# Three seams of a two-layer decoder kernel: the operands of the next stage made before the last product of the stage in front

## The chip, the cores and the metric

The kernel runs on one core of a Trainium2 chip (trn2). The metric is the device time of one execution in microseconds. PE is TensorE, ACT is ScalarE, DVE is VectorE, POOL is GpSimd, SP is SyncE; PEld rows are the loads of weights into the array, which overlap the products.

## The reference, cut to what matters

Two layers over 256 tokens of width 1024. Each layer has a mixer sub-layer and then the channel sub-layer, in which every part of the change lies:

```python
def peer_ffn(h, w_q, sk1, sk2, u_tab, v_tab):      # h: normed and modulated (adaLN) input
    q = (t @ w_q).reshape(T, PEER_HEADS, 2, PEER_DKEY // 2)
    s1 = einsum('thd,kd->thk', q[:, :, 0], sk1); s2 = einsum('thd,kd->thk', q[:, :, 1], sk2)
    v1, i1 = top_k(s1, 16); v2, i2 = top_k(s2, 16)
    vc, ic = top_k(v1[..., :, None] + v2[..., None, :], 16)      # 16 of 128*128 experts, 8 heads
    gate = softmax(vc)
    a = einsum('td,thkd->thk', t, u_tab[expert])
    return einsum('thk,thkd->td', gate * gelu(a), v_tab[expert])
```

The kernel computes it without gathering: the product of `h` with all 16384 rows of `u_tab`, gelu, a multiplication with a dense grid of gates (zero where an expert was not picked), and the product of that grid with all of `v_tab`.

## The kernel before

All weights come as a stream of 512 KB blocks (128 x 1024 float32) through a ring of four slots, `ring`; SP issues the transfer of a block when the block four places ahead of it has been used. The order of work on each engine is written out by hand, and semaphores join the engines.

Products of the channel sub-layer are exact in two halves. Each operand is split in a rounded float32r part and a remainder (`h_hi`, `h_lo`; `split_hi`, `split_lo`; `w_hi`, `w_lo`), and PE makes three products for each (hi hi, hi lo, lo hi). ScalarE makes `split_hi` of a block (`high(n)`, L685), GpSimd or VectorE subtracts to get `split_lo` (L477, L1217, L1251). There are four slots of `split_hi` and `split_lo`.

The channel sub-layer of a layer goes like this:

- **Norm (seam A).** ScalarE squares the columns of x, PE sums them (`sums_of`, L1340) and then runs 36 filler products (`keep_running`), ScalarE takes the root (L516), having first split three blocks (L685). VectorE takes the reciprocal (L878) and multiplies eight slices of x by it into `sq` (L880). For each of eight slices k, ScalarE then applies scale and shift in place in `sq` (L693), and VectorE rounds it to `h_hi` (L1146) and subtracts to get `h_lo` (L1147). PE starts the query projection with slice 0 as soon as its two halves are there; slice k is waited for by `h_split`.
- **Queries and plain expert rows.** 16 query blocks, then 64 of the 128 blocks of `u_tab` ("rows", 24 products of 256 columns each). ScalarE follows in pairs of rows: it splits two further blocks and applies gelu to the pair (`gelu_pair`). Meanwhile VectorE does the top-k. Before the last four plain rows PE turns the picks (L1705) and ScalarE copies them to `pick` (L728).
- **Late rows (seam B in front of them).** The other 64 rows, each behind a group of four gate products (`gate_grids`, L1718): four tokens at a time, a one-hot of the first index times a one-hot of the second index gives that token's grid of gates. ScalarE makes the second one-hots (`column_hots(q)`: four Abs of 128 x 128, L736, and one Relu, L739), VectorE makes the first (`row_hots(q)`, L1202) and multiplies the gates into the gelus (`weigh(q)`, L1211 and L1212). There are 64 groups q and two buffers of one-hots. `column_hots(0)` and `column_hots(1)` stand behind the last plain `gelu_pair`. The gelus of the two rows that are just done go to `late_gelu` and are multiplied in by `weigh_late` (L1226).
- **Output rows (seam C in front of them).** 128 blocks of `v_tab`, each with 12 products of 512 columns (L1751) into banks 4 to 7 of PSUM, which add up over all blocks. Before them VectorE waits for all of `weigh_late`, clears `zeros` and signals `w_done`; PE multiplies `zeros` with `xT` in plain float32 to set the four banks to zero (L1741), ScalarE makes `w_hi` of the first four blocks of weights (L766) and VectorE `w_lo` (L1246). `w_hi` and `w_lo` lie over `h_hi`. The first four `v_tab` blocks were split as the last four of the early sequence (`high`, `late_low`). In the first layer, each 20 output rows are followed by column sums for the second layer's adaLN (`ada_sums`, L1353), whose input VectorE adds up in `ada_step` from a second ring, `ada_ring`.

Of the kernel before, what the change touches and what calls it, by code (L numbers as in the profile page):

```python
# [18 lines left out]
F32 = mybir.dt.float32  # L19
# [145 lines left out]
def build(nc, stream, s5w, consts, mixc, small, vec, pos, x_in, out):  # L165
    with ExitStack() as ctx:
# [11 lines left out]
        def at_byte(name, at, shape, dt=F32):  # L178
            return nc.alloc_sbuf_tensor_at(name, [P] + shape, dt, offset=base + at, align_bytes=32)
# [11 lines left out]
        h_hi = at_byte("h_hi", 48 * KB, [KT, T], F32R)  # L191
        w_hi = at_byte("w_hi", 48 * KB, [SPLIT, T], F32R)
        w_lo = at_byte("w_lo", 52 * KB, [SPLIT, T], F32R)
        y_rows = at_byte("y_rows", 48 * KB, [TT, D])
# [9 lines left out]
        late_gelu = at_byte("late_gelu", 67 * KB, [2, 2, T])  # L204
        zeros = at_byte("zeros", 72 * KB, [P])
        ynT = at_byte("ynT", 72 * KB, [KT, T])
# [7 lines left out]
        mod2 = sb("mod2", [P, DEPTH, ADA])  # L214
        tiny = sb("tiny", [P, 216])

# [65 lines left out]
        onehot = g(120 * T, 2048)  # L282
        qT = sq

        tpos = [0]
# [21 lines left out]
        posc = tn(2)  # L307
        epst = tn(1)
        zero = tn(1)
        drel = at_byte("drel", 70 * KB + 512, [(BUCKETS - 1) * HEADS])  # L310
# [83 lines left out]
        vhi_ready, v_ready, v_used = sem("vhi_ready"), sem("v_ready"), sem("v_used")  # L394
        turned_picks, w_done = sem("turned_picks"), sem("w_done")
        spill = nc.dram_tensor("spill", (P, HEADS * (P + T) + 3 * T), F32).ap()
# [13 lines left out]
        def _(sp):  # L410
# [26 lines left out]
            for l in range(DEPTH):  # L437
# [7 lines left out]

                sp.wait_ge(w_done, l + 1)
                with sp.Fori(0, ADA // KT, 1) as i:
# [48 lines left out]
        def _(act):  # L496
# [55 lines left out]
            for l in range(DEPTH):  # L552
# [170 lines left out]
                gelus(6)  # L723
                for j in range(4):
                    if j == 2:
                        act.wait_ge(turned_picks, l + 1)
                        for i in range(TT):
                            nc.scalar.activation(pick[:, :, i * P:i * P + P], bank[:, 6 + i, 0:3 * P].rearrange("p (r t) -> p r t", r=3),  # L728
                                                 ACT.Copy).then_inc(pick_ready, 1)
                    gelu_pair(7, j)  # L730

                def column_hots(q):
# [8 lines left out]

                act.wait_ge(pick_ready, TT * (l + 1))
                for q in range(2):
                    column_hots(q)
# [41 lines left out]
        def _(dve):  # L786
# [82 lines left out]
            for l in range(DEPTH):  # L869
# [350 lines left out]
                def weigh_late(p):  # L1220
# [6 lines left out]
                        .then_inc(late_done, 1)  # L1227

                for q in range(2):
# [12 lines left out]
                v.memset(zeros[:, :], 0.0).then_inc(w_done, 1)  # L1242
                late = early_at(l) + EARLY
                for j in range(SPLIT):
                    dve.wait_ge(vhi_ready, l * KEYS + j + 1)
                    v.tensor_tensor(w_lo[:, j, :], grid[:, j * T:j * T + T], w_hi[:, j, :].bitcast(F32), ALU.subtract).then_inc(v_ready, 1)  # L1246

# [50 lines left out]
        def _(pe):  # L1298
# [79 lines left out]
            for l in range(DEPTH):  # L1378
# [358 lines left out]

                pe.wait_ge(w_done, l + 1)
                pe.wait_ge(late_lo, (l + 1) * DVE_LOWS)
                for b4 in range(4):  # L1740
                    mm(bank[:, 4 + b4, :], zeros[:, :], xT[:, 0:2, :], start=True, stop=False, skip_group_check=True)  # L1741

                def output_rows(i, n, a0):

                    for j in range(n):
                        s = (a0 + j) % SPLIT
                        pe.wait_ge(v_ready, i * n + (l * KEYS + a0 + j + 1))
                        for r in range(TT):
                            for half_w, half_v in ((w_hi, split_hi), (w_hi, split_lo), (w_lo, split_hi)):
                                for c in range(2):  # L1750
                                    last = mm(bank[:, 4 + 2 * r + c, :], half_w[:, s, r * P:r * P + P],  # L1751
                                              half_v[:, s, c * 512:c * 512 + 512], start=False, stop=False, skip_group_check=True)
                        last.then_inc(v_used, 1)

                if l + 1 < DEPTH:
                    with pe.Fori(0, ADA // KT, 1) as i:
                        output_rows(i, 20, 0)
                        pe.wait_ge(ada_used, i * KT + ((l + 1) * ADA + KT))
                        ada_sums(0, i, ada_acc)
                    output_rows(0, 8, 120)  # L1760
                else:
                    with pe.Fori(0, KEYS // SPLIT, 1) as i:
                        output_rows(i, SPLIT, 0)

# [142 lines left out]
```

## Time and profile before

| | us |
|---|---|
| median of 3 runs | 2254.84 (2251.26 to 2256.5) |
| the profiled execution, its own time | 2254.05 |
| span of the profile | 2252.3 |
| PE busy | 2140.1 (95%) |
| DVE busy | 1547.3 (69%) |
| ACT busy | 1226.8 (54%) |
| POOL busy | 440.0 (20%) |
| mean granted clock of TensorE | 0.979 of full |

The span is 1.75 us shorter than the execution's own time. The first layer's channel sub-layer runs from about 289 to 1180 us of the span, the second's from about 1358 to 2240 us. A timeline row gives start and length in us, the engine, the line, the operation, output and input, and in brackets how long the engine sat idle before it and what ended that. A group "x4" is one row for four instructions in a row.

### The profile page before, as it was taken

The page shows a single profiled execution, that of the slowest core. Times are in us where ns is not written, and L with a number is a line of the kernel's source. Part 1 is how long each engine was busy: PE and PEld are TensorE (multiplying, and loading weights), DVE is VectorE, ACT ScalarE, POOL GpSimd, SP SyncE. Part 2 cuts the span into 40 slices and gives each one's busy share as a digit, 9 for nine tenths or more (in the row PEclk, how much of TensorE's full clock was granted, in tenths as well). Part 3 has the DMA queues.
Part 4 walks back from the last instruction along what each step waited for, and adds up shares of the span by engine and source line. Part 5 has one row for each costly group of instructions (what it writes and reads, how often), then busy time and mean ns, then how long its engine had stood idle before and what let it go on. Part 6 is the DMA issues. An engine that isn't in the chain of part 4 may idle for free.

```text
span 2252.3 us, 39908 instructions
## 1 busy us (share of the span) xinstructions
PE 2140.1 (95%) x13732; PEld 1947.7 (86%) x13732; DVE 1547.3 (69%) x3026; ACT 1226.8 (54%) x2330; POOL 440.0 (20%) x184
## 2 busy tenths in 40 slices
PE   5799999999999999999999989999999999999997
PEld 4688789999999978888878978999999997888886
DVE  7688458991678867777758945899168885555555
ACT  8623434555788844444443343454578884554553
POOL 0000056898000000000000005689800000000000
PEclk9799999999999999999999999999999999999999
DMA  7723244545444457777763323445544444555552
GB/s 261 277 85 122 95 133 140 169 165 189 131 132 147 133 174 262 261 261 262 258 208 117 122 75 133 140 168 168 187 132 138 142 135 140 192 195 194 190 193 102
DMA packets 103475, 378.80 MB, mean 168 GB/s; under 512 B 11488, under 2 KB 11872, under 8 KB 102880
## 3 DMA queue, kind: packets, MB, share of 16 engines
q1 hardware_dynamic: 102672, 373.74, 49.4%
q10 hardware_dynamic: 720, 4.00, 0.5%
q8 instruction: 46, 0.75, 0.1%
q14 instruction: 37, 0.30, 0.0%
HBM read 375.46 MB, written 2.23 MB: 168 GB/s over the span
## 4 chain that ended last, share of the span: by engine, by line
PE 72%; issue 9%; POOL 7%; DVE 5%; DMA 3%; ACT 2%; SPq 0%; POOLq 0%; DVEq 0%; ACTq 0%
PE bank L1751 29%; PE bank L1654 8%; PE bank L1655 8%; PE bank L1656 8%; POOL split_lo L477 7%; PE bank L1718 5%; PE bank L1391 4%; DMA ring<-stream 2%; PE bank L1403 1%; PE bank L1642 1%; PE bank L1353 1%; DMA ada_ring<-stream 1%; DVE grid L855 1%; ACT split_hi L685 1%; PE bank L1427 1%
## 5 line engine op out<-in xcount | busy, mean ns | idle before, releaser
L1654 PE MATMUL bank<-h_hi,split_hi 128*128 128x256 f32 x2304 | 668.7, 290 | 25.2 <-POOL split_lo L477 11.1
L1655 PE MATMUL bank<-h_lo,split_hi 128*128 128x256 f32 x2304 | 653.9, 284 | 0.0
L1656 PE MATMUL bank<-h_hi,split_lo 128*128 128x256 f32 x2304 | 653.8, 284 | 0.0
L1251 DVE TENSOR_TENSOR split_lo<-ring,split_hi 128x1024 fp32r<-128x1024 f32 x248 | 303.8, 1225 | 251.3 <-ACT w_hi L773 251.3
L1654 PEld LDWEIGHTS bank<-h_hi,split_hi 128*128 128x128 f32 x2304 | 443.7, 193 | 32.0 <-POOL split_lo L477 16.8
L477 POOL TENSOR_TENSOR split_lo<-ring,split_hi 128x1024 fp32r<-128x1024 f32 x168 | 433.2, 2603 | 175.4 <-ACT split_hi L685 175.2
L772 ACT ACTIVATE split_hi<-ring 128x1024 fp32r<-128x1024 f32 x248 | 263.2, 1061 | 361.6 <-PE bank L1751 361.6
L1655 PEld LDWEIGHTS bank<-h_lo,split_hi 128*128 128x128 f32 x2304 | 444.4, 193 | 0.0
L1656 PEld LDWEIGHTS bank<-h_hi,split_lo 128*128 128x128 f32 x2304 | 443.6, 193 | 0.0
L685 ACT ACTIVATE split_hi<-ring 128x1024 fp32r<-128x1024 f32 x296 | 298.6, 1051 | 211.9 <-PE bank L1656 211.8
L1751 PE MATMUL bank<-split_hi,w_hi 128*128 128x512 f32 x1024 | 316.9, 391 | 0.0
L1751 PE MATMUL bank<-split_lo,w_hi 128*128 128x512 f32 x1024 | 315.4, 389 | 0.0
L1751 PE MATMUL bank<-split_hi,w_lo 128*128 128x512 f32 x1024 | 315.3, 389 | 0.0
L1751 PEld LDWEIGHTS bank<-split_hi,w_hi 128*128 128x128 f32 x1024 | 191.8, 188 | 40.6 <-issue 1.2
L1751 PEld LDWEIGHTS bank<-split_lo,w_hi 128*128 128x128 f32 x1024 | 192.2, 188 | 40.1
L1751 PEld LDWEIGHTS bank<-split_hi,w_lo 128*128 128x128 f32 x1024 | 192.2, 188 | 40.0
L1217 DVE TENSOR_TENSOR split_lo<-ring,split_hi 128x1024 fp32r<-128x1024 f32 x128 | 151.1, 1221 | 98.8 <-ACT split_hi L685 98.8
L470 POOL TENSOR_TENSOR tiny<-tiny,K 128x1 f32<-128x1 f32 x12 | 6.6, 549 | 1019.2 <-DVE tiny L1056 1019.2
L1202 DVE TENSOR_SCALAR hots<-K,pick 128x128 f32<-128x128 f32 x512 | 145.6, 346 | 61.9 <-ACT pick L728 61.9
L736 ACT ACTIVATE hots<-K,pick 128x128 f32<-128x128 f32 x512 | 163.6, 394 | 23.4 <-PE bank L1718 23.4
L1718 PE MATMUL bank<-hots 128*128 128x128 f32 x1024 | 136.7, 277 | 9.0 <-ACT hots L739 9.0
L1718 PEld LDWEIGHTS bank<-hots 128*128 128x128 f32 x1024 | 126.9, 193 | 9.3 <-issue 9.3
(273 smaller groups left out, 2546.2 us busy)
## 6 DMA issues: line engine op xcount, KB each, us to landing
ring<-stream SPq DMA_DIRECT2D x658, 512.0 KB, 3.4
ada_ring<-stream SPq DMA_DIRECT2D x48, 512.0 KB, 4.3
spill<-tables ACTq DMA_DIRECT2D x1, 1152.0 KB, 4.3
tables<-spill ACTq DMA_DIRECT2D x1, 1152.0 KB, 7.1
xT<-x_in SPq DMA_DIRECT2D x1, 1024.0 KB, 9.6
s5raw<-s5w ACTq DMA_DIRECT2D x2, 512.0 KB, 5.6
y_out<-hT SPq DMA_DIRECT2D x1, 1024.0 KB, 3.9
KM<-mixc SPq DMA_DIRECT2D x1, 576.0 KB, 7.6
```

Of the source, the lines that this page charges most:

```text
L477: gp.tensor_tensor(split_lo[:, j, :], ring[:, (e0 + j) % RING, :], split_hi[:, j, :].bitcast(F32), ALU.subtract)\
L685: nc.scalar.activation(split_hi[:, n % SPLIT, :], ring[:, (e0 + n) % RING, :], ACT.Copy).then_inc(hi_ready, 1)
L736: last = nc.scalar.activation(hotB[q % 2][:, t, :], iota, ACT.Abs, scale=-1.0, bias=pick[:, 1, at:at + 1])
L772: nc.scalar.activation(split_hi[:, j, :], ring[:, s, :], ACT.Copy)
L1202: last = v.tensor_scalar(hotA[q % 2][:, t, :], iota, pick[:, 0, at:at + 1], pick[:, 2, at:at + 1], ALU.is_equal, ALU.mult)
L1217: v.tensor_tensor(split_lo[:, e % SPLIT, :], ring[:, (early_at(l) + e) % RING, :], split_hi[:, e % SPLIT, :].bitcast(F32), ALU.subtract).t ...
L1251: v.tensor_tensor(split_lo[:, s, :], ring[:, (late + j) % RING, :], split_hi[:, s, :].bitcast(F32), ALU.subtract)
L1654: mm(dst, hi, x_hi, start=start, stop=False, skip_group_check=not group)
L1655: mm(dst, hi, x_lo, start=False, stop=False, skip_group_check=not group)
L1656: return mm(dst, lo, x_hi, start=False, stop=stop, skip_group_check=not group)
L1718: last = mm(bank[:, 4 + q % 4, t * P:t * P + P], hotB[q % 2][:, t, :], hotA[q % 2][:, t, :], start=True, stop=True)
L1751: last = mm(bank[:, 4 + 2 * r + c, :], half_w[:, s, r * P:r * P + P], half_v[:, s, c * 512:c * 512 + 512], start=False, stop=False, skip_g ...
```

## The change

Four edits, all in the channel sub-layer, in both layers:

1. *h in two forms.* ScalarE writes each slice twice: rounded, straight into `h_hi`, and in full into a new place `h_full`; VectorE only subtracts. The rounding on VectorE, and a wait of VectorE on itself behind it, are gone. A one-element Sqrt on ScalarE (`junk`) stands ahead of the three early splits.
2. *One-hot columns.* `column_hots(0)` and `column_hots(1)` stand ahead of the last plain `gelu_pair`.
3. *First weights' halves.* `w_hi` and `w_lo` of the first four blocks are made in the turn of the last late pair (`weights_high`, `weights_low`), behind a wait for all 64 groups of gates, and lie where the one-hots lay (72 KB).
4. *No zero products.* `zeros` and its products are gone; the first output row starts the sums. PE no longer waits for `w_done`, but for `w_ready` and block by block for `late_lo`. The first four output rows stand ahead of the loop, so the adaLN sums come after 24, 44, ... output rows. ScalarE's and SP's later parts wait for `late_done`.

```diff
@@ ScalarE
+                nc.scalar.activation(junk, epst, ACT.Sqrt)
                 for n in range(SPLIT - 1):
                     high(n)
                 root(l, "ss2", D, rstd)
                 for k in range(KT):
                     act.wait_ge(xr_ready, 2 * KT * l + KT + k + 1)
-                    nc.scalar.activation(sq[:, k, :], sq[:, k, :], ACT.Identity, bias=mod2[:, l, 3 * KT + k:3 * KT + k + 1],
-                                         scale=sc2[:, k:k + 1]).then_inc(h_ready, 1)
+                    for dst in (h_hi, h_full):
+                        last = nc.scalar.activation(dst[:, k, :], sq[:, k, :], ACT.Identity,
+                                                    bias=mod2[:, l, 3 * KT + k:3 * KT + k + 1], scale=sc2[:, k:k + 1])
+                    last.then_inc(h_ready, 1)
                 high(SPLIT - 1)
...
+                    if j == 3:
+                        act.wait_ge(pick_ready, TT * (l + 1))
+                        for q in range(2):
+                            column_hots(q)
+                    gelu_pair(7, j)
+
+                def weights_high():
+
+                    act.wait_ge(w_ready, QUADS * (l + 1))
+                    for j in range(SPLIT):
+                        nc.scalar.activation(w_hi[:, j, :], grid[:, j * T:j * T + T], ACT.Copy).then_inc(vhi_ready, 1)
...
+                    if p == LATE_PAIRS - 1:
+                        weights_high()
                     act.wait_ge(a_ready, first + FIRST_LATE // 2 + p + 1)
                     for w in range(2):
                         high(PQ + a0 + w + SPLIT)
...
-                act.wait_ge(w_done, l + 1)
+                act.wait_ge(late_done, LATE_PAIRS * (l + 1))
                 late = e0 + EARLY
-                for j in range(SPLIT):
-                    nc.scalar.activation(w_hi[:, j, :], grid[:, j * T:j * T + T], ACT.Copy).then_inc(vhi_ready, 1)
@@ VectorE
                     dve.wait_ge(h_ready, 2 * KT * l + KT + k + 1)
-                    link(v.tensor_copy(h_hi[:, k, :], sq[:, k, :]))
-                    v.tensor_tensor(h_lo[:, k, :], sq[:, k, :], h_hi[:, k, :].bitcast(F32), ALU.subtract).then_inc(h_split, 1)
+                    v.tensor_tensor(h_lo[:, k, :], h_full[:, k, :], h_hi[:, k, :].bitcast(F32), ALU.subtract).then_inc(h_split, 1)
...
+                    if p == LATE_PAIRS - 1:
+                        weights_low()
                     for w in range(2):
                         late_low(POOL_LOWS + 2 * p + w)
                     weigh_late(p)
...
-                v.memset(zeros[:, :], 0.0).then_inc(w_done, 1)
@@ TensorE
-                pe.wait_ge(w_done, l + 1)
-                pe.wait_ge(late_lo, (l + 1) * DVE_LOWS)
-                for b4 in range(4):
-                    mm(bank[:, 4 + b4, :], zeros[:, :], xT[:, 0:2, :], start=True, stop=False, skip_group_check=True)
+                pe.wait_ge(w_ready, QUADS * (l + 1))
...
+                for j in range(SPLIT):
+                    pe.wait_ge(v_ready, l * KEYS + j + 1)
+                    pe.wait_ge(late_lo, (l + 1) * DVE_LOWS - SPLIT + j + 1)
+                    output_row(j, first=j == 0)
                 if l + 1 < DEPTH:
                     with pe.Fori(0, ADA // KT, 1) as i:
-                        output_rows(i, 20, 0)
+                        output_rows(i, 20, SPLIT)
```

## Rows read from the trace of the kernel before

**Rows 1.** Page, part 1: engine, busy us, share of the span, instructions.

```profile
PE 2140.1 (95%) x13732; PEld 1947.7 (86%) x13732; DVE 1547.3 (69%) x3026; ACT 1226.8 (54%) x2330; POOL 440.0 (20%) x184
```

**Rows 2.** Windows: busy us of PE, PEld, DVE, ACT, POOL; PEclk, DMA share, GB/s.

```profile
301.00:310.00 9.00, 6.68 (x33) 5.68 (x34) 6.42 (x14) 3.09 (x5) 2.46 (x1) 0.81 0.17 60
...
570.00:807.00 237.00, 237.00 (x2016) 237.00 (x2016) 188.10 (x463) 192.16 (x429) 0.00 (x0) 1.00 0.42 137
820.00:1100.00 280.00, 280.00 (x1277) 233.24 (x1276) 198.88 (x239) 136.66 (x200) 0.00 (x0) 1.00 0.73 259
```

**Rows 3.** Timeline of the norm in the first layer (seam A).

```profile
289.76 2.93 ACT L685 ACTIVATE split_hi<-ring 128x1024 fp32r<-128x1024 f32 x3
290.88 7.17 POOL L477 TENSOR_TENSOR split_lo<-ring,split_hi 128x1024 fp32r<-128x1024 f32 x3 [29.27 <-ACT split_hi L685]
...
292.60 0.45 ACT L516 ACTIVATE grid<-bank,tiny 128x256 f32<-128x256 f32 x1
...
294.94 5.39 DVE L880 TENSOR_TENSOR grid<-xT,grid 128x256 f32<-128x256 f32 x8
...
298.36 3.55 ACT L693 ACTIVATE grid<-grid,mod,tiny 128x256 f32<-128x256 f32 x7 [1.89 <-DVE grid L880]
...
303.23 2.45 DVE L1147 TENSOR_TENSOR h_lo<-grid,h_hi 128x256 fp32r<-128x256 f32 x1
...
305.73 0.38 PE L1654 MATMUL bank<-h_hi,split_hi 128*128 128x256 f32 x1 [2.07 <-DVE h_lo L1147]
...
307.24 0.42 DVE L1147 TENSOR_TENSOR h_lo<-grid,h_hi 128x256 fp32r<-128x256 f32 x1
...
308.77 0.38 ACT L511 ACTIVATE grid<-bank 128x256 f32<-128x256 f32 x1 [5.91 <-PE bank L1656]
```

**Rows 4.** Timeline of ScalarE from the last plain pairs into the late rows, first layer.

```profile
550.33 0.86 ACT L728 ACTIVATE pick<-bank 128x384 f32<-128x384 f32 x2
...
556.26 0.58 ACT L711 ACTIVATE grid<-bank 128x512 f32<-128x512 f32 x1
...
562.49 1.26 ACT L736 ACTIVATE hots<-K,pick 128x128 f32<-128x128 f32 x4
563.78 0.63 ACT L739 ACTIVATE hots<-hots 128x512 f32<-128x512 f32 x1
...
576.30 0.16 ACT L758 ACTIVATE late_gelu<-bank 128x16 f32<-128x16 f32 x1
```

**Rows 5.** Timeline, PE's first two groups of gates: first layer, then second.

```profile
564.56 2.04 PE L1718 MATMUL bank<-hots 128*128 128x128 f32 x8 [4.49 <-ACT hots L739]
...
570.42 1.05 PE L1718 MATMUL bank<-hots 128*128 128x128 f32 x8
...
1633.52 1.64 PE L1718 MATMUL bank<-hots 128*128 128x128 f32 x8 [4.49 <-ACT hots L739]
...
1638.90 1.06 PE L1718 MATMUL bank<-hots 128*128 128x128 f32 x8
```

**Rows 6.** Timeline of seam C in the first layer.

```profile
805.64 0.16 DVE L1212 COPY grid<-bank 128x8 f32<-128x8 f32 x1
...
809.00 2.36 DVE L1217 TENSOR_TENSOR split_lo<-ring,split_hi 128x1024 fp32r<-128x1024 f32 x2 [3.20 <-ACT split_hi L685]
...
812.25 1.33 ACT L766 ACTIVATE w_hi<-grid 128x256 fp32r<-128x256 f32 x4 [1.85 <-DVE zeros L1242]
...
812.27 6.62 PE L1741 MATMUL bank<-xT,zeros 128*128 128x512 f32 x8 [4.40 <-DVE zeros L1242]
...
818.33 1.02 PE L1751 MATMUL bank<-split_hi,w_hi 128*128 128x512 f32 x2
```

**Rows 7.** Timeline of seam C in the second layer, PE alone.

```profile
1880.76 6.57 PE L1741 MATMUL bank<-xT,zeros 128*128 128x512 f32 x8 [4.40 <-DVE zeros L1242]
1886.76 1.03 PE L1751 MATMUL bank<-split_hi,w_hi 128*128 128x512 f32 x2
```

**Rows 8.** Waits of PE from 1098 to 1160 us: us in total, times, longest.

```profile
PE bank L1353 <- DVE ada_acc L1264: 1.2, 1, 1.2
```

More of the change, by code:

```diff
@@ L191, in build @@
         h_hi = at_byte("h_hi", 48 * KB, [KT, T], F32R)
-        w_hi = at_byte("w_hi", 48 * KB, [SPLIT, T], F32R)
-        w_lo = at_byte("w_lo", 52 * KB, [SPLIT, T], F32R)
+        w_hi = at_byte("w_hi", 72 * KB, [SPLIT, T], F32R)
+        w_lo = at_byte("w_lo", 76 * KB, [SPLIT, T], F32R)
         y_rows = at_byte("y_rows", 48 * KB, [TT, D])
@@ L204, in build @@
         late_gelu = at_byte("late_gelu", 67 * KB, [2, 2, T])
-        zeros = at_byte("zeros", 72 * KB, [P])
         ynT = at_byte("ynT", 72 * KB, [KT, T])
@@ L214, in build @@
         mod2 = sb("mod2", [P, DEPTH, ADA])
-        tiny = sb("tiny", [P, 216])
+        tiny = sb("tiny", [P, 217])
         g3 = grid[:, :].rearrange("p (a t) -> p a t", a=KEYS)
@@ L283, in build @@
         qT = sq
+        h_full = g(8192, KT, T)
         tpos = [0]
@@ L308, in build @@
         epst = tn(1)
+        junk = tn(1)
         zero = tn(1)
@@ L394, in build @@
         vhi_ready, v_ready, v_used = sem("vhi_ready"), sem("v_ready"), sem("v_used")
-        turned_picks, w_done = sem("turned_picks"), sem("w_done")
+        turned_picks = sem("turned_picks")
         spill = nc.dram_tensor("spill", (P, HEADS * (P + T) + 3 * T), F32).ap()
@@ L444, in _ @@
                     break
-                sp.wait_ge(w_done, l + 1)
+                sp.wait_ge(late_done, LATE_PAIRS * (l + 1))
                 with sp.Fori(0, ADA // KT, 1) as i:
@@ L723, in _ @@
                 gelus(6)
[L724 to L730, printed above, removed]
                 def column_hots(q):
@@ L740, in column_hots @@
                         .then_inc(column_ready, 1)
-                act.wait_ge(pick_ready, TT * (l + 1))
-                for q in range(2):
-                    column_hots(q)
+                for j in range(4):
+                    if j == 2:
+                        act.wait_ge(turned_picks, l + 1)
+                        for i in range(TT):
+                            nc.scalar.activation(pick[:, :, i * P:i * P + P], bank[:, 6 + i, 0:3 * P].rearrange("p (r t) -> p r t", r=3),
+                                                 ACT.Copy).then_inc(pick_ready, 1)
+                    if j == 3:
[7 more added lines that the diff above has]
+                        nc.scalar.activation(w_hi[:, j, :], grid[:, j * T:j * T + T], ACT.Copy).then_inc(vhi_ready, 1)
                 for p in range(LATE_PAIRS):
@@ L1227, in weigh_late, with weights_low @@
                         .then_inc(late_done, 1)
+                def weights_low():
+                    for j in range(SPLIT):
+                        dve.wait_ge(vhi_ready, l * KEYS + j + 1)
+                        v.tensor_tensor(w_lo[:, j, :], grid[:, j * T:j * T + T], w_hi[:, j, :].bitcast(F32), ALU.subtract)\
+                            .then_inc(v_ready, 1)
                 for q in range(2):
@@ L1241, in _ @@
                 dve.wait_ge(late_done, LATE_PAIRS * (l + 1))
-                v.memset(zeros[:, :], 0.0).then_inc(w_done, 1)
                 late = early_at(l) + EARLY
-                for j in range(SPLIT):
-                    dve.wait_ge(vhi_ready, l * KEYS + j + 1)
-                    v.tensor_tensor(w_lo[:, j, :], grid[:, j * T:j * T + T], w_hi[:, j, :].bitcast(F32), ALU.subtract).then_inc(v_ready, 1)
                 def low(i, n, j):
@@ L1736, in _, with output_row @@
                     late_rows(i, False)
-                pe.wait_ge(w_done, l + 1)
-                pe.wait_ge(late_lo, (l + 1) * DVE_LOWS)
-                for b4 in range(4):
-                    mm(bank[:, 4 + b4, :], zeros[:, :], xT[:, 0:2, :], start=True, stop=False, skip_group_check=True)
+                pe.wait_ge(w_ready, QUADS * (l + 1))
+                def output_row(s, first=False):
+                    for r in range(TT):
+                        for n, (half_w, half_v) in enumerate(((w_hi, split_hi), (w_hi, split_lo), (w_lo, split_hi))):
+                            for c in range(2):
+                                last = mm(bank[:, 4 + 2 * r + c, :], half_w[:, s, r * P:r * P + P],
+                                          half_v[:, s, c * 512:c * 512 + 512], start=first and n == 0, stop=False, skip_group_check=True)
+                    last.then_inc(v_used, 1)
@@ L1743, in output_rows @@
                 def output_rows(i, n, a0):
                     for j in range(n):
-                        s = (a0 + j) % SPLIT
                         pe.wait_ge(v_ready, i * n + (l * KEYS + a0 + j + 1))
[L1748 to L1752, printed above, removed]
@@ L1753, in output_rows @@
-                        last.then_inc(v_used, 1)
+                        output_row((a0 + j) % SPLIT)
+                for j in range(SPLIT):
+                    pe.wait_ge(v_ready, l * KEYS + j + 1)
+                    pe.wait_ge(late_lo, (l + 1) * DVE_LOWS - SPLIT + j + 1)
+                    output_row(j, first=j == 0)
                 if l + 1 < DEPTH:
                     with pe.Fori(0, ADA // KT, 1) as i:
-                        output_rows(i, 20, 0)
+                        output_rows(i, 20, SPLIT)
@@ L1758, in _ @@
                         pe.wait_ge(ada_used, i * KT + ((l + 1) * ADA + KT))
                         ada_sums(0, i, ada_acc)
-                    output_rows(0, 8, 120)
+                    output_rows(0, LATE - 120, SPLIT + 120)
                 else:
-                    with pe.Fori(0, KEYS // SPLIT, 1) as i:
-                        output_rows(i, SPLIT, 0)
+                    with pe.Fori(0, LATE // SPLIT, 1) as i:
+                        output_rows(i, SPLIT, SPLIT)
                 pe.wait_ge(y_copied, 2 * TT * (l + 1))
```

## The prediction

> **What bounds the kernel now.** I read the page first: PE is busy for 95% of the span and no other engine for more than 69% [rows 1]. So the time is PE's work plus PE's holes, and the change, which takes almost no work from PE, must be judged by the holes. The windows come second: from 570 to 807 us (late rows) and from 820 to 1100 us (output rows) PE is busy in every microsecond at a granted clock of 1.00, which is the 2.4 GHz level [rows 2]. There, nothing on another engine matters. What is left are three seams in each layer, read in the timeline.
>
> *Seam A* [rows 3]. The root ends at 293.05. VectorE's eight multiplications take 5.39 us and end at 300.33, since GpSimd's three subtractions run until 298.05; a VectorE operation of two inputs beside a GpSimd subtraction takes long (one `h_lo` took 2.45 us against 0.42). That one leaves PE idle for 2.07 us. VectorE's last `h_lo` ends at 307.66, and PE's first query row is ready for ScalarE at 308.77. From 301 to 310 us the granted clock was 0.81 on average [rows 2].
>
> *Seam B* [rows 5]. PE ends the last plain row at 564.56 - 4.49 = 560.07, waits 4.49 us for the first one-hot columns, and then runs the gates and half a row at the lower clock: the first gates take 2.04 us, the second 1.05. The second gates start at 570.42.
>
> *Seam C* [rows 6]. PE ends the last late row at 812.27 - 4.40 = 807.87, waits 4.40 us, spends 6.06 us on the zero products, and starts the output rows at 818.33.
>
> **The change part by part.**
>
> *C, no zero products and early halves.* The output rows can start when three things are there. (1) All gates weighed: `weigh(63)` ends at 805.80 [rows 6]. (2) The halves of the first weights. ScalarE's four copies take 1.33 us [rows 6] and end near 807.2; VectorE follows each with a subtraction of the shape of `h_lo`, 0.42 us [rows 3], so the first is ready near 805.85 + 0.4 + 0.42 = 806.7, the fourth near 807.7. ScalarE is idle then: it waits for the last late pair. (3) The halves of the first two `v_tab` blocks, which belong to the pair before. So PE goes on at 807.87. Blocks 2 and 3 are split at 809.00 to 811.36 as before [rows 6]; what is queued behind the new wait on `w_ready` on ScalarE are these two splits, which could not start before 807.9 anyway, since they wait for the last late row. One output row takes about 2.75 us: in 280 us there are 1277 matmul records [rows 2], of which 80 are five times the adaLN sums, so 1197/12 = 100 rows, 280/100 = 2.8 with the sums. Block 2 is needed at 807.9 + 5.5 = 813.4 and is there at 810.2; block 3 at 816.1 against 811.4. Block 4 waits for ScalarE, which waits for `late_done` (near 812), then split and copy and VectorE's two subtractions, some 3.1 us: 815.2, needed at 818.9. SP's first further transfer goes with it; it comes 7.3 us after the first output row starts, and its block is needed 22 us after. Gain: 818.33 - 807.87 = 10.46 in the first layer, 1886.76 - (1880.76 - 4.40) = 10.40 in the second [rows 7]. **20.9 us.** Its floor is the zero products alone, if PE still had to wait as long: 6.06 + 6.00 = 12.1.
>
> *B, one-hot columns early.* Picks are copied by 551.2 and ScalarE is free from 556.84, after the pair before the last [rows 4]. A set of columns takes 1.26 + 0.63 us less overlap, near 1.85: ready at 558.7 and 560.5 [rows 4]. PE needs the first at 560.07 and the second one row later. What is now queued behind the second set are the two splits of the last plain pair, which began at 560.10 and now begin at 560.5: 0.4 late, for rows that PE reaches at 568 or later; GpSimd's subtractions behind them end near 566.3. Behind the gelu of that pair (near 563) VectorE weighs group 0 and makes the row one-hots of group 2, near 565 to 566, needed at 567.9. What is saved is exact: a gate group and a row take (812.27 - 4.40 - 570.42)/63 = 3.77 us in steady work, and the second group would start at 560.07 + 3.77 = 563.84 and not at 570.42: 6.58. In the second layer 1638.90 - (1629.03 + 3.77) = 6.10 [rows 5]. **12.7 us.** Its floor is the two idle stretches without the clock's part, 9.0.
>
> *A, h in two forms.* VectorE drops eight roundings, but ScalarE now makes two activations per slice. Seven took 3.55 us [rows 3], so fourteen take 7.10; both of slice 0 fit in the gap before 298.36. ScalarE ends at 305.46. The added Sqrt is nearest to the activation of 16 columns, 0.16 us [rows 4]; below, nothing, if it overlaps. It delays the three splits, the root behind them (ScalarE goes from one to the other without a gap) and the chain: I take 0.1. The last `h_lo` ends at 305.56 + 0.42 = 306.0 instead of 307.66. The fourth split moves behind the sixteen activations (to 305.6), so GpSimd's fourth subtraction no longer meets the `h_lo` chain: the 2.45 us case is gone. Its block is needed two rows later, near 312.5, and is there near 309. Gain per layer: 1.7 by this, and up to 0.4 more if the last products run at the full clock. Against it: writes in the rounded form might not overlap as the seven did. At the full-width 0.60 each fourteen take 8.4, and the gain is 0.4. The clock is the other unknown. Before, PE worked in short bursts and the clock fell behind the 2.07 us hole. Now it gets one slice (three products) per 1.0 us for five slices. If the clock falls at the end of that, the next row runs at half speed for up to 3 us, 1.4 lost. I take 1.6 per layer, **3.2 us**; ends -2 and +5 for both layers.
>
> The Trainium skill, "TensorE: Matmul & The Clock Gate", section "A second HAM failure mode: psum-queue depth-cycling", tells of a kernel whose matmul groups had brief idles between them and whose clock went back and forth between its two levels. By this the thin stretch of seam A would end in the lower clock; that is the first rival below. The trace shows a drop only behind real holes here; a stretch fed as thinly as the new one is in no row.
>
> *adaLN sums four rows later.* One wait of 1.2 us, in the first layer's last turn, is for `ada_step` being late [rows 8]. With four more rows in front, 11 us, it goes: **1.2 us**, at worst 0. In return VectorE's first `ada_step` of the next turn waits for the sums, some 1.4 us in each of five turns; its next block is then ready some 5 us before PE needs it. No cost.
>
> **Sum.** 20.9 + 12.7 + 3.2 + 1.2 = 38.0. The profiled execution took 2254.05, which gives 2216.05. The median of the runs is 0.79 above that execution: 2216.8, rounded 2217.
>
> **The rivals.**
>
> *1. The clock falls at seam A.* Gain there between -1 and 0.3 per layer instead of 1.6: 2220 to 2222. For it: the thin feed; against it: seams A before had idles as well and recovered within 3 us.
>
> *2. The cover of seam C or B is too thin.* At C the margin between the first `w_lo` (806.7) and 807.87 is 1.2 us. If ScalarE's copies came behind the last late pair after all, PE would wait 4.4 us again in each layer and only the zero products would be saved: 2217 + 8.8 = 2226. Against it: `weigh(63)` at 805.80 in the trace.
>
> *3. The gain of B is given back in the late rows.* PE moves 6.6 us ahead of ScalarE and VectorE, which are busy for 192 and 188 of 237 us [rows 2]. If they can't follow, PE waits until the old spacing is back: 2217 + 12.7 = 2230. Against it: everything that they do is released by PE's own signals, and they have 45 us of idle time to catch up.
>
> *4. The other side: without its pauses TensorE is granted less clock.* The pauses at B and C go, and PE works without a hole from 301 to 1180 us and from 1370 to 2236 us, some 1750 us. To end slower than 2254.84 by 0.2%, 38 + 4.5 = 42.5 us must be lost: 1750 (1/x - 1) = 42.5 at a clock of x = 0.976. At 0.95 it would cost 92 us: 2309. Against it: 237 us and 280 us without any pause at 1.00 [rows 2].
>
> **How the numbers follow.** A run of this kernel tells a change of about 0.2% (4.5 us) from none. Forecast 0.66; rival 1 0.15; rival 2 0.09; rival 3 0.05; rival 4 0.04; no measurable change, by something that I don't see, 0.01. All but the last two are faster: 0.95, same 0.01, slower 0.04. The range: below, seam A at +5 (1.8 under the sum) and the spread of the runs, whose fastest is 3.6 under their median: 2211.5. Above, rival 1 and the floor of B or rival 2: 2226.
>
> **What would show it.** In the new profile: no L1741 rows; the first output product within 0.3 us of the last late product; the first gates start near 560 at 1.05 us, not at 564.56 at 2.04; all `h_lo` at 0.42 us and 16 activations in about 8 us; no wait for `ada_acc`; PE busy time some 13 us lower for the zero products, and a few us for the clock. Wrong would be: PE idle before the first output row over 1 us; a wait at the third or fifth output row; PE waits inside the late rows; granted clock under 1.00 in the long stretches.

## The result, and the profile after

The changed kernel takes 2213.76 us (median of 4 runs, 2213.12 to 2216.07); the kernel before, in the same comparison, 2253.87. The ratio is 0.9824 with a 95% interval of 0.9811 to 0.9838: 40 us faster. The forecast was 2217.0, with a range of 2211.5 to 2226. Of all executions below, one, of the version with late halves, took 11902 us; it counts in no ratio.

The page of the changed kernel, part 1 (busy us, share of the span, instructions), answers to [rows 1]:

```profile
span 2211.3 us, 39875 instructions
...
PE 2118.7 (96%) x13716; PEld 1934.7 (87%) x13716; DVE 1543.2 (70%) x3008; ACT 1234.4 (56%) x2348; POOL 440.1 (20%) x184
```

PE has 16 rows fewer, the zero products, and is busy for 21.4 us less. The span is 41.0 us shorter, so about half of it was busy time (zero products, and work at the lower clock) and half was idle.

The windows (columns as in [rows 2]) of the three seams in both layers, and of the long stretches behind them:

```profile
300.00:310.00 10.00, 8.54 (x63) 7.70 (x63) 2.48 (x7) 7.98 (x14) 4.61 (x2) 1.00 0.11 31
1347.00:1358.00 11.00, 9.39 (x57) 8.58 (x58) 2.81 (x8) 7.76 (x15) 4.72 (x2) 0.84 0.17 54
555.00:566.00 11.00, 11.00 (x96) 11.00 (x95) 6.56 (x13) 9.93 (x22) 6.32 (x3) 1.00 0.60 192
...
796.00:808.00 12.00, 12.00 (x60) 10.14 (x60) 8.21 (x12) 7.21 (x12) 0.00 (x0) 1.00 0.48 169
...
560.00:796.00 236.00, 236.00 (x2008) 236.00 (x2007) 191.42 (x469) 193.81 (x434) 2.60 (x2) 1.00 0.44 141
800.00:1150.00 350.00, 350.00 (x1593) 291.38 (x1592) 247.74 (x299) 169.34 (x248) 0.00 (x0) 1.00 0.75 261
```

Seams B (third row) and C (fourth) are full. Seam A is not: PE is idle for 1.5 us of ten in the first layer and for 1.6 of eleven in the second. The granted clock stayed at 1.00 there in the first layer and fell to a mean of 0.84 in the second.

The timeline of seam A in the first layer, against [rows 3]:

```profile
288.66 0.19 ACT L689 ACTIVATE tiny<-tiny 128x1 f32<-128x1 f32 x1
288.75 2.93 ACT L686 ACTIVATE split_hi<-ring 128x1024 fp32r<-128x1024 f32 x3
289.87 7.18 POOL L478 TENSOR_TENSOR split_lo<-ring,split_hi 128x1024 fp32r<-128x1024 f32 x3 [29.62 <-ACT split_hi L686]
...
293.94 5.41 DVE L891 TENSOR_TENSOR grid<-xT,grid 128x256 f32<-128x256 f32 x8
...
303.78 0.58 ACT L696 ACTIVATE grid<-grid,mod,tiny 128x256 f32<-128x256 f32 x1
...
304.40 0.43 DVE L1157 TENSOR_TENSOR h_lo<-grid,h_hi 128x256 fp32r<-128x256 f32 x1 [0.56 <-ACT grid L696]
...
305.54 0.38 ACT L512 ACTIVATE grid<-bank 128x256 f32<-128x256 f32 x1 [0.22 <-PE bank L1671]
```

The last `h_lo` ends 16.5 us behind the last square (start 288.34), where it took 18.2 before (307.66 - 289.44). ScalarE sets the pace: the last activation ends and the last subtraction starts 0.04 us later. VectorE's eight multiplications still take 5.4 us beside GpSimd.

Seam B in the first layer, ScalarE and VectorE, then PE, against [rows 4, 5]:

```profile
553.04 1.27 ACT L732 ACTIVATE hots<-K,pick 128x128 f32<-128x128 f32 x4
554.35 0.63 ACT L735 ACTIVATE hots<-hots 128x512 f32<-128x512 f32 x1
...
556.72 1.99 ACT L686 ACTIVATE split_hi<-ring 128x1024 fp32r<-128x1024 f32 x2
...
559.97 3.23 DVE L1212 TENSOR_SCALAR hots<-K,pick 128x128 f32<-128x128 f32 x4
```

```profile
556.21 1.06 PE L1733 MATMUL bank<-hots 128*128 128x128 f32 x8
...
559.98 1.06 PE L1733 MATMUL bank<-hots 128*128 128x128 f32 x8
563.75 1.06 PE L1733 MATMUL bank<-hots 128*128 128x128 f32 x8
```

The columns are ready before PE ends its plain rows, the first gates run at the full clock, and the groups follow each other at 3.77 us from the first. The VectorE row is the close one: four row one-hots took 3.23 us beside GpSimd's subtractions (one of the four alone 2.44) and ended at 563.20, for gates at 563.75. The second layer has the same margin of 0.55 us.

Seam C in the first layer, against [rows 6]:

```profile
795.20 0.16 DVE L1222 COPY grid<-bank 128x8 f32<-128x8 f32 x1
795.85 1.43 DVE L1243 TENSOR_TENSOR w_lo<-grid,w_hi 128x256 fp32r<-128x256 f32 x4 [0.48 <-ACT w_hi L754]
798.57 2.36 DVE L1227 TENSOR_TENSOR split_lo<-ring,split_hi 128x1024 fp32r<-128x1024 f32 x2 [1.29 <-ACT split_hi L686]
```

```profile
797.28 0.63 PE L1760 MATMUL bank<-split_hi,w_hi 128*128 128x512 f32 x2
```

All four `w_lo` are there at 797.28, when PE begins its output rows, and PE waits for none of them.

**Where the 41.0 us of the span went.** The same marks are read in both timelines: last square, ScalarE's copy of the second query row, copy of the picks, first `late_gelu`, copy of the finished sums to `y_rows`.

| stretch | layer 1: before, after | layer 2: before, after | gain |
|---|---|---|---|
| last square to second query row (A) | 22.65, 20.07 | 22.28, 21.55 | 3.3 |
| to the copy of the picks | 238.24, 238.23 | 238.41, 238.37 | 0.1 |
| to the first late gelu (B) | 25.97, 19.22 | 25.48, 19.23 | 13.0 |
| to the finished sums (C and the adaLN sums) | 603.34, 590.88 | 590.77, 579.80 | 23.4 |

Ahead of the first square, between the layers and behind the last sums, where nothing was changed, the two profiles differ by 1.1 us together, nearly all of it at the start. That makes 40.9, the 41.0 of the span but for rounding.

The table sets one execution against one. How long the kernel before takes at seams A and C differs from profile to profile. Over the ten profiled layers with the old seam A (before, b_only, c_only, b_fill, b_fill18) the stretch takes 22.3 to 23.3 us, 22.8 in the mean; over the ten with h in two forms and late early splits (after, a_only, halves_late, four_back, no_sqrt) it takes 20.0 to 21.6, 20.5 in the mean. So edit 1 is worth some 4.6 us for both layers, and the 3.3 of this pair is at the low end.

### The profile page after: what moved, and what is told of

The parts are those of the page before. It is cut to its first block, busy times and chain, and to the rows that moved or that the text cites. A ratio compares the mean times of both kernels' runs of the same rounds, so it can differ in the third digit from the quotient of the medians.

```text
span 2211.3 us, 39875 instructions
## 1 busy us (share of the span) xinstructions
PE 2118.7 (96%) x13716; PEld 1934.7 (87%) x13716; DVE 1543.2 (70%) x3008; ACT 1234.4 (56%) x2348; POOL 440.1 (20%) x184
## 4 chain that ended last, share of the span: by engine, by line
PE 74%; issue 9%; POOL 8%; DVE 4%; ACT 2%; DMA 2%; POOLq 0%; ACTq 0%; SPq 0%; DVEq 0%
PE bank L1760 32%; PE bank L1669 8%; PE bank L1670 8%; PE bank L1671 8%; POOL split_lo L478 7%; PE bank L1733 5%; PE bank L1406 4%; DMA ring<-stream 2%; PE bank L1418 1%; PE bank L1657 1%; PE bank L1368 1%; ACT diag L536 1%; PE bank L1431 1%; PE bank L1442 1%; PE bank L1379 1%
## 5 line engine op out<-in xcount | busy, mean ns | idle before, releaser
L1669 PE MATMUL bank<-h_hi,split_hi 128*128 128x256 f32 x2304 | 666.5, 289 | 23.3 <-POOL split_lo L478 11.1
L1212 DVE TENSOR_SCALAR hots<-K,pick 128x128 f32<-128x128 f32 x512 | 150.4, 360 | 61.9 <-ACT pick L742 61.9
```

The lines of the kernel that those rows point to most:

```text
L1212: last = v.tensor_scalar(hotA[q % 2][:, t, :], iota, pick[:, 0, at:at + 1], pick[:, 2, at:at + 1], ALU.is_equal, ALU.mult)
L1669: mm(dst, hi, x_hi, start=start, stop=False, skip_group_check=not group)
```

## The experiments

All ratios are against the kernel before, run on the same chip. A stretch is named by the letters of the table.

**Each part alone.** Edit 1 in the kernel before (h in two forms and the Sqrt; the diffs are cut to what matters):

```diff
+                    for dst in (h_hi, h_full):
+                        last = nc.scalar.activation(dst[:, k, :], sq[:, k, :], ACT.Identity, ...)
+                    last.then_inc(h_ready, 1)
```

> Edit 1 alone (h in two forms, with the one-element Sqrt) in the kernel before. Theory 1, each part fills its own hole in PE's work and the parts add: the profiles of before and after give 2.6 us in the first layer and 0.8 in the second, 3.4 together, so a ratio near 0.9985. Theory 2, the parts share a gain (PE arriving earlier at one seam waits longer at the next): the holes at seams B and C would be longer than 4.49 and 4.40 us and nothing would be left, ratio 1.000. The clock: if the thin feed of slices alone is enough to lower it, the query row after seam A runs at the lower clock in at least one layer.

Measured: 2247.55 us, ratio 0.9974 (0.9962 to 0.9985). A is 20.07 in both layers, 4.8 us less together, more than expected: this time the clock did not fall in either layer, so the query row at the lower clock, which was expected in at least one, did not come. C did not change its length before the first weights' halves (235.96 from the first late gelu, against 235.95), so nothing is given back there. B is 26.49 and 26.46, 0.5 to 1.0 longer than before, at the same wait.

Edit 2 in the kernel before:

```diff
+                    if j == 3:
+                        act.wait_ge(pick_ready, TT * (l + 1))
+                        for q in range(2):
+                            column_hots(q)
                     gelu_pair(7, j)
```

> Edit 2 alone (one-hot columns ahead of the last plain gelus). Theory 1: 6.75 + 6.25 = 13.0 us, ratio 0.9942, and the hole at seam C stays at 4.40 us. Theory 2 (given back in the late rows or at seam C): the hole at C grows by what B gained, ratio over 0.998.

Measured: 2240.46 us, ratio 0.9945 (0.9929 to 0.9962). B is 19.22 in both layers, and the stretch from the first late gelu to the first weights' halves is 235.96, as in the kernel before. That is theory 1: nothing is given back.

Edits 3 and 4, by undoing 1 and 2 in the changed kernel:

```diff
-                    if j == 3:
-                        act.wait_ge(pick_ready, TT * (l + 1))
-                        for q in range(2):
-                            column_hots(q)
                     gelu_pair(7, j)
+                act.wait_ge(pick_ready, TT * (l + 1))
+                for q in range(2):
+                    column_hots(q)
```

> Edits 3 and 4 alone (halves of the first weights early, no zero products, adaLN sums after 24, 44, ... rows). Theory 1: 10.6 + 10.6, 0.4 per layer for the first products at the full clock and 1.2 to 1.5 for the adaLN sum, 23.2 us, ratio 0.9897. Theory 2: under 15 us, ratio over 0.993, with new waits of PE inside the first output rows.

Measured: 2229.54 us, ratio 0.9894 (0.9878 to 0.9911). C is 590.88 and 579.81, as in the changed kernel to 0.01 us. The three parts sum to 4.8 + 13.0 + 23.4 = 41.2 us by their stretches; together they gave 39.7. The difference of 1.5 us is seam A of the second layer, where the clock fell.

**The two halves of seam C.** Halves of the first weights behind the last late pair, still without zero products:

```diff
                 act.wait_ge(late_done, LATE_PAIRS * (l + 1))
+                weights_high()
@@ and on VectorE
                 dve.wait_ge(late_done, LATE_PAIRS * (l + 1))
+                weights_low()
```

> The changed kernel, but the halves of the first weights made after the last late pair again; the zero products stay out. It tells the two halves of seam C apart. Theory 1: PE waits from the last late product for the last multiplication of the late pair (4.1 us) and then for one copy and one subtraction (1 us), 5.2 us a layer, and starts at the lower clock for 2 to 3 us (1 to 1.5 more): 12 to 13 us slower than the changed kernel, ratio to before 0.988. Theory 2, that the zero products were the whole price and the early halves are worth nothing: same as the changed kernel, 0.982.

Measured: 2228.13 us, ratio 0.9887 (0.9867 to 0.9906). C is 6.8 and 7.0 us longer than in the changed kernel, 13.8 together. PE's timeline in the first layer:

```profile
803.81 1.20 PE L1758 MATMUL bank<-split_hi,w_hi 128*128 128x512 f32 x2 [5.17 <-issue]
804.80 1.06 PE L1758 MATMUL bank<-split_lo,w_hi 128*128 128x512 f32 x2
805.65 1.06 PE L1758 MATMUL bank<-split_hi,w_lo 128*128 128x512 f32 x2
...
807.55 0.62 PE L1758 MATMUL bank<-split_hi,w_lo 128*128 128x512 f32 x2
```

A hole of 5.17 us, and then pairs of products at 1.06 us until the clock is back and they take 0.62. The first output row (twelve products) takes 4.20 and 4.40 us, against 2.75 in the changed kernel. So each layer loses the hole and 1.45 to 1.65 us of lower clock behind it. Without the early halves, edits 3 and 4 are worth 9.6 of the 23.4 us, the adaLN sums' 1.4 included.

**The price of the four products.** In front of the output rows of the changed kernel:

```diff
+                for b4 in range(4):
+                    mm(bank[:, 4 + b4, :], ident, xT[:, 0:2, :], start=True, stop=True)
```

> The changed kernel with four plain float32 products of the shape of the zero products back in front of the output rows (operands: the identity and x; the first output row overwrites what they leave, so the sums are those of the changed kernel). It prices the four products when PE comes to them at the full clock. Before they took 6.06 us behind a hole. Theory 1: their price was mostly the lower clock, so here 3.0 to 3.5 us a layer, 6 to 7 us in all over the changed kernel, ratio to before 0.985. Theory 2, their price doesn't hang on the clock: 12 us, ratio 0.9876.

Measured: 2221.95 us, ratio 0.9854 (0.9837 to 0.987). C is 3.46 us longer in each layer (594.34 and 583.26). PE's timeline in the first layer:

```profile
799.12 3.60 PE L1755 MATMUL bank<-xT,K 128*128 128x512 f32 x8
802.15 1.02 PE L1762 MATMUL bank<-split_hi,w_hi 128*128 128x512 f32 x2
```

From the start of the four products to the start of the first output product it is 3.03 us. The other 0.42 lies in the first output product, which has to let the last of the four end: the first pair takes 1.02 us here, as it did behind the zero products [rows 6], and 0.63 in the changed kernel. The lower clock is not the reason, in neither kernel. The windows of the kernel before (columns as in [rows 2]), over the zero products and from the first output product on:

```profile
812.00:818.00 6.00, 5.73 (x7) 2.52 (x8) 1.60 (x5) 1.33 (x4) 0.00 (x0) 0.50 0.46 160
818.30:821.50 3.20, 3.20 (x15) 2.44 (x13) 0.00 (x0) 0.00 (x0) 0.00 (x0) 1.00 0.00 0
```

So at the full clock four plain float32 products of 512 columns cost 3.46 us. Behind the hole of the kernel before they cost 6.06 [rows 6] and the same 0.42, 6.5 in all. In the ten profiled layers with zero products, always behind 4.40 us of idle time, start to start they took 4.65 to 6.06 us, by how much of them ran at the lower clock. So of the 13 us that the zero products cost in the first profile, 6 belonged to the hole in front of them.

**The clock at seam B.** Filler products in the hole of the kernel before, first 36, then 18:

```diff
+                for _ in range(36):
+                    mm(bank[:, 4, 0:P], ident, ones, start=True, stop=True)
                 late_rows(0, True)
```

> The kernel before with 36 filler products of 128 columns in the hole of seam B (bank 4, which the first gates overwrite), nothing moved. It splits B's gain into the wait and the clock. Theory 1: the wait of 4.49 us stays, but the first gates and the first late row run at the full clock: 2.1 + 1.6 = 3.7 us less, ratio 0.9984. Theory 2, the clock's part is no part of its own: ratio 1.000.

Measured: 2256.52 us, ratio 1.0009 (1.0000 to 1.0019), a miss by a wrong count: a plain float32 product stands as two rows in the profile, so the fillers lasted not 4.1 but 8.2 us and became the path themselves. B is 27.26 in both layers. The norm's own 36 fillers had stood as 72 rows and 8.20 us in the trace of the kernel before.

```profile
562.51 8.20 PE L1735 MATMUL bank<-K 128*128 128x128 f32 x72
570.55 1.06 PE L1718 MATMUL bank<-hots 128*128 128x128 f32 x8
```

> The kernel before with 18 filler products (36 rows of 0.114 us, 4.1 us) in the hole of seam B, half of what stood in the run with 36, whose 72 rows took 8.2 us and were longer than the hole. Theory 1, seam B is a wait of 4.49 us plus the lower clock behind it: the stretch from the copy of the picks to the first late gelu, 25.5 to 26.5 us before and 19.2 after, is 19.2 + 4.5 = 23.7 here in both layers. Theory 2, the clock has no part: 25.5 or more.

Measured: 2250.2 us, ratio 0.9983 (0.9974 to 0.9993). B is 23.95 and 23.96, against 25.5 to 26.5 in the six profiled layers where this seam was neither filled nor moved (before, a_only and c_only) and 19.22 with early columns. With the fillers the granted clock of the seam is 1.00. So seam B was a wait of 4.7 us and 1.5 to 2.5 us of lower clock behind it. The numbers of the two theories lay apart, and the first holds.

**The one-element Sqrt.** Taken out of the changed kernel:

```diff
-                nc.scalar.activation(junk, epst, ACT.Sqrt)
```

> The changed kernel without the one-element Sqrt. Theory 1: no table load hangs on it (none stands before the root of this norm in either profile), so it costs its 0.1 us a layer: same as the changed kernel, root 0.1 us earlier. Rival: without it a load of 1.28 us appears before the root, 2.6 us slower.

Measured: 2213.83 us, ratio 0.9811 (0.9794 to 0.9827). The root comes 3.17 us behind the last square and not 3.25, and there is no table load in front of it in either kernel. It costs 0.1 us a layer and gives nothing. A in the second layer is 21.47: the clock fell here too.

**GpSimd beside VectorE.** The three early splits between the last squares:

```diff
+                for m in range(KT):
+                    act.wait_ge(dve_taken, taken_count(l, f"out{m}")[1])
+                    nc.scalar.activation(sq[:, m, :], xT[:, m, :], ACT.Square).then_inc(sq_ready, 1)
+                    if m >= 5:
+                        if l == 0 and m == 5:
+                            act.wait_ge(spilled, 16)
+                        high(m - 5)
                 nc.scalar.activation(junk, epst, ACT.Sqrt)
-                for n in range(SPLIT - 1):
-                    high(n)
```

> The changed kernel with the three early splits of ScalarE spread between the last squares instead of behind them (and the Sqrt left out of the way of the root is gone with them only in place: it now stands behind the squares). GpSimd then ends its three subtractions before VectorE's eight multiplications. Theory 1, VectorE is held up by GpSimd: the eight take 2.7 us instead of 5.4, ScalarE's first gap goes, and seam A ends 1.5 to 2 us earlier in each layer: 3 to 4 us less than the changed kernel, ratio 0.9808. Rival: ScalarE waits for a block at its ring slot and delays the squares, so that nothing is won: 0.9824.

Measured: 2206.88 us, ratio 0.9789 (0.9773 to 0.9805). Its timeline in the first layer:

```profile
290.32 2.35 POOL L478 TENSOR_TENSOR split_lo<-ring,split_hi 128x1024 fp32r<-128x1024 f32 x1 [1.11 <-ACT split_hi L681]
...
294.19 2.77 DVE L892 TENSOR_TENSOR grid<-xT,grid 128x256 f32<-128x256 f32 x8
```

GpSimd is through before VectorE begins, the eight multiplications take 2.77 us and not 5.41, and A is 17.79 in both layers: 2.3 us less than the undisturbed 20.07. The median is 6.9 us below the changed kernel's, where 3 to 4 were expected: in the profiles 4.6 are these two stretches, and 1.5 the clock, which did not fall in either layer here.

With that in place, the first edit undone:

```diff
-                    for dst in (h_hi, h_full):
-                        last = nc.scalar.activation(dst[:, k, :], sq[:, k, :], ACT.Identity, ...)
+                    nc.scalar.activation(sq[:, k, :], sq[:, k, :], ACT.Identity, ...).then_inc(h_ready, 1)
@@ and on VectorE
+                    link(v.tensor_copy(h_hi[:, k, :], sq[:, k, :]))
```

> The changed kernel with the early splits, but h in one form (edit 1 undone, no Sqrt). It tells whether edit 1 is worth anything when GpSimd's first three subtractions are out of the way. Theory 1, half of edit 1's gain was that GpSimd's fourth subtraction no longer met the h_lo chain: here it meets it again (ScalarE is through after 8 activations, near 299.7, and GpSimd starts while VectorE has four slices to go), one h_lo takes 2.4 us, and seam A is 1 to 2 us longer than with both: 18.9 to 19.8. Rival: VectorE's 0.66 us per slice beats ScalarE's 0.98 and seam A is 0.9 us shorter: 16.9.

Measured: 2213.6 us, ratio 0.9821 (0.9805 to 0.9838). A is 20.39 in both layers, 2.6 longer than with two forms. The row that decides:

```profile
298.24 2.37 POOL L478 TENSOR_TENSOR split_lo<-ring,split_hi 128x1024 fp32r<-128x1024 f32 x1 [7.04 <-ACT split_hi L681]
298.38 2.51 DVE L1156 TENSOR_TENSOR h_lo<-grid,h_hi 128x256 fp32r<-128x256 f32 x1
```

The fourth GpSimd subtraction meets the `h_lo` chain again: one subtraction takes 2.51 us, and the query row behind it 3.82 us instead of 2.88, by the clock. So what counts in edit 1 is the moved fourth split, and not ScalarE's speed: in one form the last `h_lo` ends 15.5 us behind the last square, of which some 2.1 are the held subtraction, and in two forms 14.2. No run moves the fourth split alone, so that one form would then be the shorter is worked out and not shown.

And the odd slices rounded by VectorE, the even ones in two forms by ScalarE (with the early splits, without the Sqrt):

```diff
+ROUNDED = (0, 2, 4, 6)
...
+                    for dst in ((h_hi, h_full) if k in ROUNDED else (h_full,)):
@@ and on VectorE
+                    if k not in ROUNDED:
+                        link(v.tensor_copy(h_hi[:, k, :], h_full[:, k, :]))
```

> The changed kernel with the early splits spread between the squares, without the Sqrt, and with h_hi of the odd slices rounded by VectorE as before (even slices in two forms by ScalarE). Theory 1, with GpSimd out of the way seam A is paced by ScalarE's 16 activations of 0.49 us: twelve of them end 2 us earlier, VectorE needs 4 x 0.34 + 4 x 0.66 = 4.0 us, last h_lo 1.7 us earlier than with the early splits alone (17.79 from the last square to the second query row): 16.1. Rival: VectorE's own wait behind each rounding or GpSimd's fourth subtraction takes it back: 17.8 or more.

Measured: 2207.27 us, ratio 0.9793 (0.9777 to 0.981). A is 16.71 and 16.72, 1.1 us shorter than with the early splits alone; 0.6 of the expected 1.7 is missing. The last `h_lo` does come 1.64 us earlier (12.56 us behind the last square, not 14.20), but PE has no idle time left between the slices, and its own work sets the end. The gain of 2.2 us does not show in the medians. In the two profiled executions the stretch between the layers, where the two kernels are the same, took 178.92 and 177.23 us, which hides it there; the medians are of four runs each, on two chips, and can't tell. Both versions beat the changed kernel by 6.5 to 7 us.

## Why the prediction was right

The direction, the size (40 measured, 38 forecast) and the order of the parts were right; term by term:

- **C: 20.9 forecast.** The stretch from the first late gelu to the first output product fell by 10.61 and 10.57 us, 21.2. The early halves were ready before PE, as computed; no block was late. A term was 0.4 us a layer too small: I took the zero products from start to start, 6.06 us, and their last one still ran beside the first output product. The clock has no part in these 0.4 us. In the kernel before it was back at the full level when the output rows began, and the first output row took 3.17 us there, as it does behind the four products put back at the full clock, against 2.75 in the changed kernel. The "floor" of the zero products alone, 12.1, was too high: alone they are worth some 8 (the 9.6 of the run with late halves less the adaLN sums), since the hole stays in front of the first output row and grows from 4.40 to 5.17 us, and the lower clock behind it, which the zero products had borne, falls on the output rows (1.45 to 1.65 us a layer).
- **B: 12.7 forecast, 13.0 measured.** That ScalarE was idle enough and the picks early enough held: the first columns were there 1.2 us before PE needed them, where I had 1.4. One step was too kind: I had the row one-hots of group 2 ready some 2 us before PE needs them. They took 3.23 us beside GpSimd instead of 1.1 to 2.1, and the margin was 0.55 us.
- **A: 3.2 forecast, 3.3 measured,** but as two unlike layers, 2.6 and 0.7, and with luck in the pair: over all profiled layers the edit is worth 4.6. The last `h_lo` came 1.7 us earlier, as computed. Behind it the first layer kept the full clock, and the second ran most of its second query row at the lower one: that row took 3.96 us and not 2.87. The term that was too small is "up to 0.4 more if the last products run at the full clock". In all ten profiled layers with the old seam the clock fell in the hole of 2.07 us or just behind it, and the second query row took 2.95 to 4.25 us: 0.1 to 1.4 more than at the full clock, beside the 0.4 in the first query row.
- **adaLN sums: 1.2 forecast, 1.4 measured.** In the first layer the stretch from the first output product to the finished sums fell by 1.84 us, of which 0.42 is the end of the zero products. The 1.4 is of this pair of profiles: in the five profiles with the old order PE waits for `ada_acc` 1.17, 0.23, 0, 1.53 and 0.12 us (before, a_only, b_only, b_fill, b_fill18), and in the last two the clock fell behind it, so that the order cost 0 to 5.0 us. In the changed kernel the wait is gone, as in all seven other profiles with the new order, and the new wait of VectorE for the sums delayed nothing.
- **The median.** From the sum of the stretches (39.8) the forecast would have been 2215.0. The rest is 1.3 us; 1.0 of it is that the kernel before took 2253.87 in the comparison and not the 2254.84 that I had started from.

**The rivals.** Rival 1, the lower clock at seam A, came true in one layer of two. Of the ten profiled layers with slices at 0.98 us and late early splits (after, a_only, halves_late, four_back, no_sqrt) the clock fell in three, at a price of 1.45 to 1.5 us each. Even so the second layer gained 0.7 us, not the -1 to 0.3 of rival 1, because the old seam had paid for the clock too. The rule of the Trainium skill ("TensorE: Matmul & The Clock Gate", "A second HAM failure mode: psum-queue depth-cycling"), that brief idles between groups of products can make the clock change level, agrees with that; that it does so in three layers of ten and not in all is this case's own finding. What decides in which is not settled: it was not tried, and a profile of each kernel shows only two such seams. The prediction says that the trace shows a drop only behind real holes. That holds at the three seams of the kernel before, in the hole or behind it, and not in all of its trace: the clock was also lower from 1214 us on, where PE had just run 32 products of 8 columns and had not been idle for more than 0.39 us at a time.

```profile
1206.00:1214.00 8.00, 7.61 (x51) 6.77 (x49) 5.36 (x5) 4.84 (x6) 0.00 (x0) 1.00 0.30 109
1214.00:1217.00 3.00, 3.00 (x11) 2.55 (x11) 2.62 (x7) 0.18 (x1) 0.00 (x0) 0.52 0.05 11
```

Rival 2 is what the run with late halves shows, 13.8 us and not the 8.8 that I had for it: the hole is 5.17 us and not 4.40, and the first output row behind it runs at the lower clock. Rivals 3 and 4 fell: each part alone keeps its gain, and a stretch of 350 us without a pause has a granted clock of 1.00.

## What to carry to other kernels

When one engine is busy for 95% of the time, price the seams between stages, and price each hole twice: the idle time, and the work behind it at the lower clock (at seam B 4.5 us of waiting cost 6.2 to 7.3). Operands of the next stage can be made in the idle time of other engines one step ahead of the last product, if what they wait for is already done; compare the ready time with the need, and count on the slower duration of a VectorE operation that will run beside GpSimd. Before adding work to one engine to relieve another, look whether the other was slow or only held up: moving three GpSimd subtractions out of VectorE's way gave 2.3 us a layer with no work added.

## What was not expected of the hardware

- A VectorE operation on two SBUF tensors (128x256) took 2.45 to 2.51 us beside a GpSimd subtraction and 0.42 without; it ended 0.3 us behind that subtraction. Four tensor-scalar operations of 128x128 took 3.23 us beside it and 1.11 without: one of the four took 2.44.
- Four plain float32 products of 512 columns cost 3.46 us at the full clock and 6.5 behind a hole of 4.40 us in the first profile. Each stands as two rows in the profile, also when it has 128 columns (72 rows for 36 products, 8.20 us).
- The same seam, fed at the same pace, kept the full clock in seven layers and lost it in three. With the hole of 2.07 us that the old seam had, it was lost in ten of ten. And 32 products of 8 columns were followed by the lower clock with no hole over 0.39 us in front.
